# The opening of a two-block transformer kernel: five feature groups run together in place of four, modulation blocks in two banks, the first block loaded ahead of the tokens

## The chip, the cores and the metric

The kernel runs on one core of a Trainium2 chip. The metric is the device time of one execution in microseconds; for the kernel before, three runs gave a median of 2280.69 us (2280.24 to 2281.05).

## The reference

Two blocks of a small transformer are computed one after the other on 256 tokens of width 1024, with 256 context tokens beside them, all in float32. The change lies in the first steps of the first block:

```
silu_c, silu_cc = silu(c), silu(c_ctx)
mod_x = silu_c @ w_mod + b_mod            # shift, scale and gate, 3 x 1024
mod_c = silu_cc @ w_mod + b_mod           # the same for the context
hn = rms_norm(h) * gain * (1 + scale) + shift      # for tokens and context
proj = hn @ w_in                          # q, k, v, two small gates, z, u, z_pool
qkv = silu(short_conv(qkv)); q, k = l2_norm(q), l2_norm(k)
... a gated delta rule in chunks, pooling, the output product
```

After it come a second block with feed-forward layers, a short convolution and attention. None of that is touched.

## The kernel before, in words

**Data.** Tokens and context stand as `h`, 8 feature tiles (k = 0 to 7) of 128 features by 512 columns. Weights come as a stream of chunks, each of 8 tiles of 128x128, through a ring of three slots (`w_raw`). To reach float32 precision, each operand is split in a high and a low part: ScalarE casts a chunk to `w_hi` (`split_ahead`, line 867), and VectorE (for the first four chunks, `low_chunk`, line 994) or GpSimd (later, line 575) subtracts to get `w_lo`. A product of one weight tile is then three matmuls (lines 603, 604 and 607: low weights by high tokens, high by high, high by low). The tokens are split the same way: scaled by VectorE (`nt`, line 1009), shifted and cast by ScalarE (`n_hi`, line 940), and the low part by VectorE (`n_lo`, line 964).

**The modulation in the opening.** Before a feature tile k can be scaled, its shift and scale have to be known. They come in five blocks (`BLOCK_TILES`: 1, 1, 2, 2 and 2 tiles of k). Per block: SP loads the weights in two halves (`load_block`, line 467), TensorE sums them into a bank (`mod_block`, line 889), ScalarE copies the sums to `mod_row` (`copy_block`, line 930), TensorE transposes them (`turn_block`, line 898), VectorE adds the bias and forms the gain (`block_gain`, lines 978 to 987). The sums of the tokens' squares are formed beside them: squares on ScalarE and VectorE (lines 924, 955), sums on TensorE (line 905), mean and reciprocal on VectorE (lines 957, 958), square root on ScalarE (line 934), spread on TensorE (line 913).

**The groups.** The input projection ("in") makes 51 groups of output features, each the sum over the 8 tiles k. The first `IN_FIRST` groups run together, so that TensorE takes tile k for all of them before it needs tile k+1; the chunks' tiles are laid out in that order. Later groups run one at a time, 8 products each. The calls of `before(g, k)` place the modulation work among the products: for k = 0, 2 and 4, blocks 2, 3 and 4 are summed at group 2 and turned at group 3. Blocks 0 and 1 are done in `pe_start`, ahead of the products. `after(g)` is called for each group once its products are issued, or for all groups of a joint part when that part is through; it calls `post(g - POST_LAG)` with `POST_LAG = 4`. For the first eight feature tiles `post` sums squares (line 1132) and waits for `tile_sq`, which comes by way of ScalarE (line 1242), VectorE (four steps of line 1302) and ScalarE again (lines 1193 and 1198).

**Order.** Each engine runs its instructions in the order written. SP issues the transfers in the order of `sp_program`. The waits are semaphores written by hand.

Of the kernel before, what the change touches and what calls it, by code (L numbers as in the profile page):

```python
# [158 lines left out]
        self.groups, self.k = groups, k  # L159


FFN_FIRST, SC_FIRST, IN_FIRST, OUT_FIRST, MLA_FIRST = 4, 5, 4, 6, 4


def mark_plan():
# [57 lines left out]
def two_block_kernel(nc, stream, modstream, tokens, ctx2, conds, cols_in, consts_in, rope_tab, count_in, out):  # L223
# [271 lines left out]

    def sp_program(sp):
        sp.dma_start(cond[:], conds[:]).then_inc(cond_in, 16)
        for part in range(2):
            sp.dma_start(h[:, 4 * part:4 * part + 4, :], tokens[:, 4 * part:4 * part + 4, :]).then_inc(tokens_in[part], 16)
        sp.dma_start(cols[:], cols_in[:]).then_inc(const_in, 16)  # L500
        sp.dma_start(consts[:, 0:2, :], consts_in[:, 0:2, :]).then_inc(const_in, 16)
        load_block(sp, 0)
        load_chunk(sp, 0, 0)
        load_block(sp, 1)
        load_chunk(sp, 1, 1)
        load_block(sp, 2)
        load_chunk(sp, 2, 2)
        load_block(sp, 3)
        sp.wait_ge(w_lo_ready, 1)
        load_chunk(sp, 3, 0)  # L510
        load_block(sp, 4)
        stream_loads(sp, FIRST_LOWS, 2 * RING)
        sp.dma_start(consts[:, 2:, :], consts_in[:, 2:, :]).then_inc(masks_in, 16)
        sp.dma_start(inv_cnt[:], count_in[:]).then_inc(masks_in, 16)
        stream_loads(sp, 2 * RING, IN_LOADS)
        sp.wait_ge(normed, KT)
        sp.dma_start(h[:, :, L:T], ctx2[:]).then_inc(ctx2_in, 16)


        sp.wait_ge(mod_used, MOD_EARLY)  # L520
        for r in range(MOD_LATE - MOD_EARLY):
            if r == 3:
                sp.wait_ge(w_lo_ready, IN_LOADS)
            if r >= RECUR_RING:
                sp.wait_ge(mod_used, MOD_EARLY + r - RECUR_RING + 1)
            load_mod(sp, MOD_EARLY + r)


        sp.wait_ge(mod_used, MOD_LATE)
        for i in range(IN_LOADS, IN_LOADS + RING):  # L530
            load_chunk(sp, i, i % RING)
        sp.wait_ge(d_o, 8)
        for q in range(7):
            load_late(sp, q)
        stream_loads(sp, IN_LOADS + RING, CH_OUT + 10)
        sp.wait_ge(y_lo_ready, 8)
        for q in (7, 8):
            load_late(sp, q)
        stream_loads(sp, CH_OUT + 10, CH_OUT + 12)
        q = LATE_RING  # L540
        for i in range(12, 16):
            load_late(sp, q)
            q += 1
            stream_loads(sp, CH_OUT + i, CH_OUT + i + 1)
        stream_loads(sp, CH_OUT + 16, CH_FFN[0] + RING)
        for q in range(q, MOD_PARTS):
            load_late(sp, q)
        q = MOD_PARTS


        at = CH_FFN[0] + RING
        for first, after, turn in ((CH_FFN[0], CH_SC, ("sc", 0)), (CH_SC, CH_FFN[1], ("ffn", 1)),
                                   (CH_FFN[1], CH_FFN[2], ("ffn", 2)), (CH_FFN[2], CH_MLA, ("mla", 0))):
            stream_loads(sp, at, first + 12)
            at = first + 12
            for _ in range(sum(LATE_TURNS[turn][:3])):
                load_late(sp, q)
                q += 1
                stream_loads(sp, at, at + 1)
                at += 1  # L560
        stream_loads(sp, at, CH_MLA + RING)
        at = CH_MLA + RING
        for n in (1, 2, 5):
            for _ in range(n):
                load_late(sp, q)
                q += 1
            stream_loads(sp, at, at + 1)
            at += 1
        assert MOD_LATE + q == MOD_END
        stream_loads(sp, at, N_STREAM)  # L570
# [298 lines left out]

    def block_room_turned(b):  # L870

        room = bank[(MOD_BANK, 4, 5, MOD_BANK, 4)[b]]
        at = (0, 0, 0, L, L)[b]
        return room[:, at:at + P], room[:, at + P:at + 2 * P]

    def block_row(b):
        at = b % 4 * P
        return mod_row[:, at:at + P]

    def mod_block(pe, b):  # L880

        pe.wait_ge(mod_full[b], 32)
        n = BLOCK_TILES[b]
        sums, _ = block_room_turned(b)
        for k in range(KT):
            for half_ in range(2):
                for sub in range(n):
                    q = 2 * half_ + (sub if n == 2 else k % 2)
                    last = nc.tensor.matmul(sums[32 * q:32 * q + 32], cond[:, 0, k, :],
                                            block_room(b)[:, half_, k, sub * P:(sub + 1) * P],  # L890
                                            start=(k < 3 - n), stop=(k >= KT - 3 + n))
        last.then_inc(mod_used, 2 * n)
# [5 lines left out]
        nc.tensor.transpose(turned, block_row(b), C(Const.IDENT)).then_inc(mod_turned, 1)  # L898

    def pe_start(pe):  # L900
        pe.wait_ge(const_in, 16 * 2)
        for k in range(KT):
            pe.wait_ge(first_sq[k % 2], k // 2 + 1)
            for t in range(4):
                last = nc.tensor.matmul(bank[MISC_BANK][32 * t:32 * t + 32, 0:P], col(Cols.SEL + 7, 32),
                                        n_space[:, 0, k, tok(t)], start=(k == 0), stop=(k == KT - 1))
        last.then_inc(sum_ready, 1)
        pe.wait_ge(cond_ready, 1)
        mod_block(pe, 0)
        turn_block(pe, 0)  # L910
        pe.wait_ge(rstd_ready, 1)
        for t in range(4):
            last = nc.tensor.matmul(bank[MISC_BANK][:, tok(t)], C(Const.IDENT)[:, 32 * t:32 * t + 1].to_broadcast([P, P]),
                                    rstd[:, 0:P], start=True, stop=True)
        last.then_inc(rstd_spread, 1)
        mod_block(pe, 1)
        turn_block(pe, 1)

    def act_start(act):
        act.wait_ge(cond_in, 16)  # L920
        nc.scalar.activation(cond[:], cond[:], ACT.Silu).then_inc(cond_ready, 1)
        for k in range(0, KT, 2):
            act.wait_ge(tokens_in[k // 4], 16)
            nc.scalar.activation(n_space[:, 0, k, :], h[:, k, :], ACT.Square).then_inc(first_sq[0], 1)

        def copy_block(b):
            act.wait_ge(mod_used, 2 * (BLOCK_FIRST[b] + BLOCK_TILES[b]))
            if b == 4:
                act.wait_ge(mod_turned, 1)
            nc.scalar.copy(block_row(b), block_room_turned(b)[0]).then_inc(mod_copied, 1)  # L930

        nc.scalar.activation(rstd[0:1, T - 1:T], h[0:1, 0, 0:1], ACT.Sqrt, scale=0.0)
        act.wait_ge(ms_ready, 1)
        nc.scalar.activation(rstd[:, 0:P], rstd[:, 0:P], ACT.Sqrt).then_inc(rstd_ready, 1)
        copy_block(0)
        split_ahead(act, -2)
        for k in range(KT):
            act.wait_ge(scaled, k + 1)
            for c, s_ in sides(T):
                last = nc.scalar.activation(n_hi[:, k, s_], nt[:, k % 2, s_], ACT.Identity,  # L940
                                            bias=mods[:, NORMS[0][1] + k, c:c + 1])
            last.then_inc(norm_hi, 1)
            if k == 0:
                copy_block(1)
                split_ahead(act, -1)
            elif k in (1, 3, 5):
                copy_block(k // 2 + 2)
                if k > 1:
                    split_ahead(act, k // 2 - 1)

    def dve_start(dve):
        gain, shift, scale = NORMS[0]
        for k in range(1, KT, 2):
            dve.wait_ge(tokens_in[k // 4], 16)
            nc.vector.tensor_tensor(n_space[:, 0, k, :], h[:, k, :], h[:, k, :], ALU.mult).then_inc(first_sq[1], 1)
        dve.wait_ge(sum_ready, 1)
        step(nc.vector.tensor_scalar(rstd[:, 0:P], bank[MISC_BANK][:, 0:P], 1.0 / D, EPS, ALU.mult, ALU.add))
        nc.vector.reciprocal(rstd[:, 0:P], rstd[:, 0:P]).then_inc(ms_ready, 1)
        dve.wait_ge(const_in, 16 * 2)

        def low(k):
# [33 lines left out]
                                    ALU.subtract).then_inc(w_lo_ready, 1)  # L995

        for b in range(MOD_BLOCKS):
            if b >= 2:
                low_chunk(b - 1)
            block_gain(b)  # L1000
            if b == 0:
                low_chunk(0)
                dve.wait_ge(rstd_spread, 1)
            tiles = range(BLOCK_FIRST[b], BLOCK_FIRST[b] + BLOCK_TILES[b])
# [6 lines left out]
                last.then_inc(scaled, 1)  # L1011
            for k in tiles:
                low(k)


    TAIL = 1 + 3 * HEADS
# [83 lines left out]
    def pe_in(pe):  # L1100
        operands = pe_operands(pe, 0, "in", L)

        def before(g, k):
            if k in (0, 2, 4):
                if g == 2:
                    mod_block(pe, k // 2 + 2)
                if g == 3:
                    turn_block(pe, k // 2 + 2)
            if (g, k) == (IN_FIRST, 0):
                pe.wait_ge(mod_ready, MOD_BLOCKS)  # L1110
            return operands(g, k)
# [69 lines left out]
    def act_in(act):  # L1181
# [37 lines left out]
            act.wait_ge(ab_act, 3)  # L1219
            nc.scalar.activation(e_tail[:], e_tail[:], ACT.Ln, bias=1.0).then_inc(ab_act, 1)  # L1220

        split = [2]

        def split_through(i):
            while split[0] <= min(i, N_IN - 1):
# [1929 lines left out]
```

## Time and profile before

| | |
|---|---|
| median of three runs | 2280.69 us |
| the profiled execution's own time | 2278.36 us |
| its span in the trace | 2276.2 us |
| TensorE busy | 2209.8 us (97%) |
| VectorE, ScalarE, GpSimd busy | 841.8, 792.9, 1013.2 us |
| mean granted clock of TensorE | 0.995 |

The span runs from the first to the last recorded instruction of one execution. Times in the rows below count from its start. The granted clock is a share of TensorE's full speed: 1.00 stands for 2.4 GHz, 0.50 for 1.2 GHz.

### The profile page before, as it was taken

To read this page: it belongs to the slowest core of one execution; us is meant where nothing else is said; L and a number is where in the kernel's file an instruction comes from. 1 tells how busy PE (TensorE), PEld (TensorE's weight loads), DVE (VectorE), ACT (ScalarE), POOL (GpSimd) and SP (SyncE) were. 2 spreads that over 40 slices of the span, in tenths; PEclk is the share of its full clock that TensorE was granted. 3 is DMA by queue.
4 is the path that set the end of the run, shared out by engine and by line. 5 is a ranking of instruction groups with operands and counts; after the bars stand their busy time and mean duration, and the time that the engine had idled before them with its cause. 6 is when DMAs were issued, how large, how long until landed. Compare 5 with 4: busy or idle time off the path is not lost.

```text
span 2276.2 us, 37013 instructions
## 1 busy us (share of the span) xinstructions
PE 2209.8 (97%) x14686; PEld 1796.9 (79%) x14686; DVE 841.8 (37%) x1519; ACT 792.9 (35%) x1264; POOL 1013.2 (45%) x469
## 2 busy tenths in 40 slices
PE   6999999989999999999999999999999999899999
PEld 5789867778778888878878888887888887658999
DVE  4566556565511311344471131133122114662212
ACT  3445434433432132232233222223222222555443
POOL 0357622344344444434444444443444443305888
PEclk9999999999999999999999999999999999999999
DMA  8235476355443223325325323332433324304556
GB/s 284 93 103 158 134 265 218 142 200 187 175 150 118 93 93 94 99 76 175 94 70 168 104 93 93 94 97 80 171 94 93 93 93 133 105 19 122 185 185 185
DMA packets 90930, 297.55 MB, mean 131 GB/s; under 512 B 8992, under 2 KB 21664, under 8 KB 90400
## 3 DMA queue, kind: packets, MB, share of 16 engines
q1 hardware_dynamic: 90640, 295.05, 39.7%
q8 instruction: 117, 1.92, 0.3%
q10 hardware_dynamic: 144, 0.34, 0.1%
q14 instruction: 29, 0.24, 0.0%
HBM read 294.31 MB, written 1.05 MB: 130 GB/s over the span
## 4 chain that ended last, share of the span: by engine, by line
issue 55%; POOL 23%; PE 16%; DVE 2%; DMA 1%; ACT 1%; SPq 1%; POOLq 1%; DVEq 0%; ACTq 0%
POOL w_lo L575 23%; PE bank L603 3%; PE bank L607 3%; PE bank L604 3%; PE bank L647 2%; PE bank L1642 1%; PE bank L1653 1%; DVE gdn_outer L2012 1%; PE bank L1621 1%; PE bank L1095 1%; PE bank L1558 1%; DMA first_mods<-in_modstream 1%; DMA mod_raw<-in_modstream 0%; DVE gdn_outer L2014 0%; PE bank L1665 0%
## 5 line engine op out<-in xcount | busy, mean ns | idle before, releaser
L575 POOL TENSOR_TENSOR w_lo<-w_raw,w_hi 128x1024 fp32r<-128x1024 f32 x379 | 922.6, 2438 | 1083.6 <-ACT w_hi L867 1083.2
L603 PE MATMUL bank<-n_hi,w_lo 128*128 128x512 f32 (+1 forms) x2216 | 789.2, 356 | 9.0 <-POOL w_lo L575 5.5
L607 PE MATMUL bank<-n_lo,w_hi 128*128 128x512 f32 (+1 forms) x2216 | 781.8, 353 | 1.5 <-DVE n_lo L778 1.3
L604 PE MATMUL bank<-n_hi,w_hi 128*128 128x512 f32 (+1 forms) x2216 | 781.0, 352 | 0.0
L867 ACT CAST w_hi<-w_raw 128x1024 fp32r<-128x1024 f32 x383 | 401.2, 1049 | 757.8 <-PE bank L607 732.5
L603 PEld LDWEIGHTS bank<-n_hi,w_lo 128*128 128x128 f32 x2216 | 415.9, 188 | 87.2 <-issue 14.3
L607 PEld LDWEIGHTS bank<-n_lo,w_hi 128*128 128x128 f32 x2216 | 415.9, 188 | 67.9 <-DVE n_lo L778 2.5
L604 PEld LDWEIGHTS bank<-n_hi,w_hi 128*128 128x128 f32 x2216 | 416.1, 188 | 62.9
L2409 DVE TENSOR_TENSOR prod<-silu,bank 128x512 f32<-128x512 f32 (+1 forms) x88 | 54.7, 622 | 717.3 <-PE bank L607 710.1
L603 PE MATMUL bank<-g_hi,w_lo 128*128 128x512 f32 (+1 forms) x768 | 283.3, 369 | 2.1 <-DVE g_lo L2400 2.1
L607 PE MATMUL bank<-g_lo,w_hi 128*128 128x512 f32 (+1 forms) x768 | 283.3, 369 | 0.0
L604 PE MATMUL bank<-g_hi,w_hi 128*128 128x512 f32 (+1 forms) x768 | 282.8, 368 | 0.0
L2368 DVE SCALAR_TENSOR_TENSOR h<-bank,gates,h 128x256 f32<-128x256 f32 x136 | 60.7, 480 | 314.5 <-PE bank L607 314.5
L603 PEld LDWEIGHTS bank<-g_hi,w_lo 128*128 128x128 f32 x768 | 144.0, 188 | 29.7 <-DVE g_lo L2400 2.5
L604 PEld LDWEIGHTS bank<-g_hi,w_hi 128*128 128x128 f32 x768 | 144.0, 188 | 27.2
L607 PEld LDWEIGHTS bank<-g_lo,w_hi 128*128 128x128 f32 x768 | 144.0, 187 | 27.2
L2354 ACT ACTIVATE silu<-bank 128x512 f32<-128x512 f32 (+1 forms) x88 | 47.8, 544 | 287.6 <-PE bank L607 287.6
L2400 DVE TENSOR_TENSOR g_lo<-prod,g_hi 128x512 fp32r<-128x512 f32 (+1 forms) x88 | 84.7, 964 | 2.4 <-ACT g_hi L2344 2.2
L1302 DVE SCALAR_TENSOR_TENSOR conv<-bank,cols,conv 128x508 f32<-128x508 f32 (+3 forms) x96 | 63.0, 659 | 49.5 <-ACT conv L1242 46.9
L1944 POOL TENSOR_TENSOR gdn_t<-gdn_inner,consts 128x256 f32<-128x256 f32 x16 | 11.7, 728 | 137.5 <-DVE gdn_inner L1997 137.5
L847 DVE TENSOR_TENSOR nt<-h 128x512 f32<-128x512 f32 (+1 forms) x56 | 58.2, 1039 | 1.9
L832 ACT ACTIVATE n_hi<-nt,mods 128x256 fp32r<-128x256 f32 x88 | 40.3, 503 | 39.3 <-DVE nt L791 39.3
(385 smaller groups left out, 1878.8 us busy)
## 6 DMA issues: line engine op xcount, KB each, us to landing
w_raw<-in_stream SPq DMA_DIRECT2D x383, 512.0 KB, 3.6
late<-in_modstream SPq DMA_DIRECT2D x56, 512.0 KB, 4.5
mod_raw<-in_modstream SPq DMA_DIRECT2D x48, 512.0 KB, 6.0
w_raw<-in_modstream SPq DMA_DIRECT2D x48, 512.0 KB, 6.1
first_mods<-in_modstream SPq DMA_DIRECT2D x6, 1024.0 KB, 11.0
h<-in_tokens SPq DMA_DIRECT2D x2, 1024.0 KB, 6.3
first_mods<-in_modstream SPq DMA_DIRECT2D x4, 512.0 KB, 8.2
consts<-in_consts SPq DMA_DIRECT2D x1, 1152.0 KB, 5.8
```

The source lines that it names most:

```text
L575: nc.gpsimd.tensor_tensor(w_lo[:, slot, :], w_raw[:, slot, :], w_hi[:, slot, :].bitcast(F32), ALU.subtract).then_inc(w_lo_ready, 1)
L603: nc.tensor.matmul(out_ap, wl, hi, start=start, stop=False)
L604: nc.tensor.matmul(out_ap, wh, hi, start=False, stop=False)
L607: return nc.tensor.matmul(out_ap, wh, lo, start=False, stop=stop)
L647: last = nc.tensor.matmul(bank[MOD_BANK][32 * j:32 * j + 32, :], cond[:, which, k, :], room[:, jj * 512:(jj + 1) * 512], start=(k == 0), s ...
L847: square = nc.vector.tensor_tensor(nt[:, k % 2, s_], h[:, k, s_], h[:, k, s_], ALU.mult)
L867: nc.scalar.copy(w_hi[:, c % RING, :], w_raw[:, c % RING, :]).then_inc(w_hi_ready, 1)
L1302: ins = nc.vector.scalar_tensor_tensor(acc[:, :, to], src[:, :, of], col(Cols.CONV + ci * CONV + j), acc[:, :, to], ALU.mult, ALU.add)
L2354: nc.scalar.activation(silu[:, f % 2, 0:w], bank[(g0 + g) % BANKS][:, 0:w], ACT.Silu).then_inc(gate_ready, 1)
L2368: last = nc.vector.scalar_tensor_tensor(h[:, d, s_], bank[g % BANKS][:, s_], gates[:, gate, d, c:c + 1], h[:, d, s_], ALU.mult, ALU.add)
L2400: nc.vector.tensor_tensor(g_lo[:, f, 0:w], prod[:, f % 2, 0:w], g_hi[:, f, 0:w].bitcast(F32), ALU.subtract).then_inc(hid_lo, 1)
L2409: nc.vector.tensor_tensor(prod[:, f % 2, 0:w], silu[:, f % 2, 0:w], bank[g % BANKS][:, 0:w], ALU.mult).then_inc(groups_read, 2)
```

## The change

The first joint part of the projection takes five groups in place of four. In SP's order, block 0 goes ahead of the small constants, and both ahead of the tokens. The modulation blocks alternate between banks 6 and 5, in two halves of each. TensorE sums and turns block 0 before the sums of squares; ScalarE copies it before its squares, and VectorE forms its gain before its squares. Block 1 goes from `pe_start` to the joint part: blocks 1 to 4 are summed at group 2 and turned at group 4 of k = 0, 1, 3 and 5. From block 2 on, TensorE waits for the gain of the block two before. ScalarE casts chunks 1 to 4 at k = 0, 2, 4 and 5, chunk 1 before the copy of block 1; chunk 4's cast comes from the part after. VectorE's `low_chunk` calls stand at the end of a block in place of the start of the next, which is the same order.

```
-FFN_FIRST, SC_FIRST, IN_FIRST, OUT_FIRST, MLA_FIRST = 4, 5, 4, 6, 4
+FFN_FIRST, SC_FIRST, IN_FIRST, OUT_FIRST, MLA_FIRST = 4, 5, 5, 6, 4
...
     def sp_program(sp):
         sp.dma_start(cond[:], conds[:]).then_inc(cond_in, 16)
+        load_block(sp, 0)
+        sp.dma_start(cols[:], cols_in[:]).then_inc(const_in, 16)
+        sp.dma_start(consts[:, 0:2, :], consts_in[:, 0:2, :]).then_inc(const_in, 16)
         for part in range(2):
             sp.dma_start(h[:, 4 * part:4 * part + 4, :], tokens[:, 4 * part:4 * part + 4, :]).then_inc(tokens_in[part], 16)
-        sp.dma_start(cols[:], cols_in[:]).then_inc(const_in, 16)
-        sp.dma_start(consts[:, 0:2, :], consts_in[:, 0:2, :]).then_inc(const_in, 16)
-        load_block(sp, 0)
         load_chunk(sp, 0, 0)
...
-        room = bank[(MOD_BANK, 4, 5, MOD_BANK, 4)[b]]
-        at = (0, 0, 0, L, L)[b]
+        room = bank[(MOD_BANK, IN_FIRST)[b % 2]]
+        at = b // 2 % 2 * L
...
+    BLOCK_STEPS = (0, 1, 3, 5)
+
     def mod_block(pe, b):
 
         pe.wait_ge(mod_full[b], 32)
+        if b >= 2:
+            pe.wait_ge(mod_ready, b - 1)
...
     def pe_start(pe):
+        pe.wait_ge(cond_ready, 1)
+        mod_block(pe, 0)
         pe.wait_ge(const_in, 16 * 2)
+        turn_block(pe, 0)
...
         last.then_inc(sum_ready, 1)
-        pe.wait_ge(cond_ready, 1)
-        mod_block(pe, 0)
-        turn_block(pe, 0)
         pe.wait_ge(rstd_ready, 1)
...
         last.then_inc(rstd_spread, 1)
-        mod_block(pe, 1)
-        turn_block(pe, 1)
...
             if k == 0:
+                split_ahead(act, -1)
                 copy_block(1)
-                split_ahead(act, -1)
             elif k in (1, 3, 5):
                 copy_block(k // 2 + 2)
-                if k > 1:
-                    split_ahead(act, k // 2 - 1)
+                if k == 5:
+                    split_ahead(act, 2)
+            elif k in (2, 4):
+                split_ahead(act, k // 2 - 1)
...
         def before(g, k):
-            if k in (0, 2, 4):
+            if k in BLOCK_STEPS:
                 if g == 2:
-                    mod_block(pe, k // 2 + 2)
-                if g == 3:
-                    turn_block(pe, k // 2 + 2)
+                    mod_block(pe, BLOCK_STEPS.index(k) + 1)
+                if g == 4:
+                    turn_block(pe, BLOCK_STEPS.index(k) + 1)
```

## Rows read from the trace of the kernel before

**Rows 1.** The page's part 1: engine, busy us, share of the span, instructions.
```profile
PE 2209.8 (97%) x14686; PEld 1796.9 (79%) x14686; DVE 841.8 (37%) x1519; ACT 792.9 (35%) x1264; POOL 1013.2 (45%) x469
```

**Rows 2.** Timeline of TensorE, opening: start us, us, line, operation, count, idle before.
```profile
10.08 3.64 PE L905 MATMUL bank<-n_space,cols 128*32 128x128 f32 x64 [10.08 <-DMA consts<-in_consts]
...
18.41 1.08 PE L889 MATMUL bank<-first_mods,cond 128*32 128x128 f32 x32 [1.50 <-DMA first_mods<-in_modstream]
...
20.84 0.50 PE L607 MATMUL bank<-n_lo,w_hi 128*128 128x512 f32 x1
...
26.86 3.64 PE L889 MATMUL bank<-first_mods,cond 128*32 128x128 f32 x64 [4.84 <-DMA first_mods<-in_modstream]
...
31.88 0.29 PE L898 MATMUL bank<-consts,mod_row 128*128 128x128 f32 x1
...
36.99 1.96 PE L889 MATMUL bank<-first_mods,cond 128*32 128x128 f32 x64
...
52.72 0.47 PE L603 MATMUL bank<-n_hi,w_lo 128*128 128x512 f32 x1 [0.45 <-ACT n_hi L940]
...
53.88 0.40 PE L603 MATMUL bank<-n_hi,w_lo 128*128 128x512 f32 x1
...
58.78 0.39 PE L603 MATMUL bank<-n_hi,w_lo 128*128 128x512 f32 x1
...
64.48 1.06 PE L1132 MATMUL bank<-act_out,cols 128*32 128x128 f32 x8
```

**Rows 3.** Stretches: from:to, us, busy us of each engine, PEclk, DMA share, GB/s.
```profile
25.60:31.80 6.20, 4.94 (x67) 4.03 (x68) 0.00 (x0) 0.27 (x1) 0.00 (x0) 0.50 1.09 354
1971.00:1974.00 3.00, 2.48 (x12) 2.19 (x11) 2.96 (x2) 2.60 (x8) 3.00 (x2) 0.50 0.03 11
2091.40:2094.40 3.00, 3.00 (x25) 3.00 (x26) 0.37 (x1) 1.32 (x3) 3.00 (x2) 1.00 0.56 161
```

**Rows 4.** The chain of waits, opening: the issue of block 0's second half.
```profile
3.98 2.78 SPq L467
```

**Rows 5.** DMA issues from 6.7 to 6.9 us: size, us from issue to landing.
```profile
first_mods<-in_modstream SPq DMA_DIRECT2D x1, 512.0 KB, 9.6
```

**Rows 6.** Timeline of VectorE, opening.
```profile
9.02 1.29 DVE L955 TENSOR_TENSOR n_space<-h 128x512 f32<-128x512 f32 x2 [1.22 <-DMA h<-in_tokens]
13.79 0.29 DVE L957 TENSOR_SCALAR rstd<-bank 128x128 f32<-128x128 f32 x1 [3.48 <-PE bank L905]
...
16.92 1.22 DVE L994 TENSOR_TENSOR w_lo<-w_raw,w_hi 128x1024 fp32r<-128x1024 f32 x1
18.06 0.87 DVE L1009 SCALAR_TENSOR_TENSOR nt<-h,gains,bank 128x256 f32<-128x256 f32 x2
...
20.96 0.23 DVE L983 TENSOR_TENSOR mods<-bank,mods 128x2 f32<-128x2 f32 x2
...
32.20 0.23 DVE L978 TENSOR_TENSOR mods<-bank,cols 128x4 f32<-128x4 f32 x2 [6.85 <-PE bank L898]
...
50.23 0.22 DVE L978 TENSOR_TENSOR mods<-bank,cols 128x4 f32<-128x4 f32 x2
...
52.61 1.68 DVE L964 SCALAR_TENSOR_TENSOR n_lo<-nt,mods,n_hi 128x256 fp32r<-128x256 f32 x4 [0.20 <-ACT n_hi L940]
```

**Rows 7.** Timeline of ScalarE, opening.
```profile
15.53 1.05 ACT L867 CAST w_hi<-w_raw 128x1024 fp32r<-128x1024 f32 x1
...
51.66 1.71 ACT L940 ACTIVATE n_hi<-nt,mods 128x256 fp32r<-128x256 f32 x4 [2.61 <-DVE nt L1009]
...
56.88 0.68 ACT L1235 ACTIVATE gb<-bank,cols 64x512 f32<-64x512 f32 x1 [1.62 <-PE bank L607]
...
62.10 0.64 ACT L1198 ACTIVATE act_out<-kT 128x512 f32<-128x512 f32 x1
```

**Rows 8.** Timeline of TensorE, two waits in later stages.
```profile
1970.59 0.54 PE L603 MATMUL bank<-c_hi,w_lo 128*128 128x256 f32 x1 [1.88 <-ACT n_space L2740]
...
2091.38 0.39 PE L603 MATMUL bank<-n_hi,w_lo 128*128 128x256 f32 x1 [2.46 <-POOL w_lo L575]
```

More of the change, by code:

```diff
@@ L921, in act_start @@
         nc.scalar.activation(cond[:], cond[:], ACT.Silu).then_inc(cond_ready, 1)
-        for k in range(0, KT, 2):
-            act.wait_ge(tokens_in[k // 4], 16)
-            nc.scalar.activation(n_space[:, 0, k, :], h[:, k, :], ACT.Square).then_inc(first_sq[0], 1)
         def copy_block(b):
@@ L930, in copy_block @@
             nc.scalar.copy(block_row(b), block_room_turned(b)[0]).then_inc(mod_copied, 1)
+        copy_block(0)
+        for k in range(0, KT, 2):
+            act.wait_ge(tokens_in[k // 4], 16)
+            nc.scalar.activation(n_space[:, 0, k, :], h[:, k, :], ACT.Square).then_inc(first_sq[0], 1)
         nc.scalar.activation(rstd[0:1, T - 1:T], h[0:1, 0, 0:1], ACT.Sqrt, scale=0.0)
@@ L934, in act_start @@
         nc.scalar.activation(rstd[:, 0:P], rstd[:, 0:P], ACT.Sqrt).then_inc(rstd_ready, 1)
-        copy_block(0)
         split_ahead(act, -2)
@@ L943, in act_start @@
             if k == 0:
+                split_ahead(act, -1)
                 copy_block(1)
-                split_ahead(act, -1)
             elif k in (1, 3, 5):
                 copy_block(k // 2 + 2)
-                if k > 1:
-                    split_ahead(act, k // 2 - 1)
+                if k == 5:
+                    split_ahead(act, 2)
+            elif k in (2, 4):
+                split_ahead(act, k // 2 - 1)
     def dve_start(dve):
         gain, shift, scale = NORMS[0]
[L953 to L958, printed above, removed]
         dve.wait_ge(const_in, 16 * 2)
@@ L997, in dve_start @@
         for b in range(MOD_BLOCKS):
-            if b >= 2:
-                low_chunk(b - 1)
             block_gain(b)
             if b == 0:
+                for k in range(1, KT, 2):
+                    dve.wait_ge(tokens_in[k // 4], 16)
+                    nc.vector.tensor_tensor(n_space[:, 0, k, :], h[:, k, :], h[:, k, :], ALU.mult)\
+                        .then_inc(first_sq[1], 1)
+                dve.wait_ge(sum_ready, 1)
+                step(nc.vector.tensor_scalar(rstd[:, 0:P], bank[MISC_BANK][:, 0:P], 1.0 / D, EPS, ALU.mult, ALU.add))
+                nc.vector.reciprocal(rstd[:, 0:P], rstd[:, 0:P]).then_inc(ms_ready, 1)
                 low_chunk(0)
@@ L1013, in dve_start @@
                 low(k)
+            if 1 <= b < FIRST_LOWS:
+                low_chunk(b)
     TAIL = 1 + 3 * HEADS
@@ L1220, in decay_and_beta @@
             nc.scalar.activation(e_tail[:], e_tail[:], ACT.Ln, bias=1.0).then_inc(ab_act, 1)
-        split = [2]
+        split = [3]
         def split_through(i):
```

## The prediction

> **What bounds the kernel now.** I read the page's busy times first, then TensorE's timeline over the first 66 us beside those of ScalarE and VectorE, then the chain of waits and the granted clock of short stretches. TensorE is busy for 2209.8 of 2276.2 us [rows 1]: whatever makes it stand anywhere comes out at the end, and no other engine has less slack. The change touches only the opening, so the question is how long TensorE stands before it has finished the groups that run together, against now.
>
> Now its first matmul starts at 10.08, on the arrival of the constants. A product is three matmuls of 512 columns; the third one of the first product starts at 20.84. After two products TensorE stands for 4.84 us until the third modulation block (tiles 2 and 3) has arrived at 26.86, and the granted clock then is 0.50, the 1.2 GHz level [rows 2, 3]: 6.20 us at that level cost about 3.1. From 31.88 to 52.72 the listing has only waits of half a microsecond, such as the 0.45 before k=6 at 52.72. Second product of k=6: 53.88; joint part over, fifth group begins: 58.78; seven products lie between, 0.70 us each [rows 2]. From there TensorE runs without a gap worth naming.
>
> I take 53.88 as the mark. By then 25 products and all blocks are done. With five groups the same point (second product of k=6) has 31 products behind it, so 53.88 + 6 × 0.70 = 58.1 would be neutral: the total of products is unchanged.
>
> **Start.** Block 0 goes ahead of the tokens on SP's queue. The issue of its second half took 2.78 us at 3.98, and that half landed 9.6 us after its start, at 13.6 [rows 4, 5]. The bytes up to there are the same in either order, so in the new order the second half of the tokens lands at about 13.6 where VectorE has it at 9.02 now [rows 6]. The constants also pass behind block 0, but have landed before the tokens. If the 2.78 us issue holds the tokens back as well, up to 0.6 more; I take 0. Then come VectorE's two squares (1.29 in all), one k of sums at the early pace (10.08 row: 64 matmuls in 3.64, so 8 in 0.46) and a handover: the mean square starts at 15.4, now 13.79. What followed it now was the square root, the row copy of block 0, and the cast of chunk 0 at 15.53 [rows 7]; without the copy (0.16 of that) the cast starts at 17.0. It takes 1.05, the low half and the scaled tokens follow 1.14 apart as now (16.92 to 18.06), so the scaling starts at 19.2, 1.14 later than now. The gain of block 0 leaves this chain, but the tokens, now last, are in it. The first product's third matmul moves from 20.84 to 22.0 and the second product ends at 23.0.
>
> Sums and turn of block 1 (1.08 us and some 0.3 as at 31.88) lay before the first product; they now lie inside k=0. ScalarE's cast of chunk 1 (1.05) is put before the copy of block 1; it would hold that up only if the chunk landed after 23.0, at worst with block 2, which is behind it in SP's queue, at 26.86 (3.9 us). I take nothing, since two 1 MB halves lie between. The other casts, the low halves on VectorE (same order as now) and the new wait for the gain of block b-2 (products queue behind it, but that gain is two blocks old) I cost at nothing too; one exception below.
>
> **The blocks.** This is the first term. From turn to use: turn at 31.88, bias add on VectorE at 32.20; later block, bias add at 50.23, first product at 52.72: 0.32 + 2.49 = 2.81 us, with nothing else on those engines in the way [rows 2, 6]. A block of one tile adds twice: 0.26 more (20.96 row). The first product after such a wait takes 1.16 (52.72 to 53.88) as its third matmul waits for the low half. Now a block summed at k=2 is used at k=4, a whole k later, and the chain is hidden but for 0.45. In the new order blocks 1, 2, 3, 4 are summed in k=0, 1, 3, 5 at the third group and turned at the fifth, and used in the next k. After the turn there is one product (0.7) to hide 2.81.
>
> Step by step, blocks of two tiles 1.96 [rows 2]: block 1 summed by 24.1, two products to 25.5, turn, k=1 starts at 25.5 + 3.07 = 28.6 (TensorE free at 26.3: 2.2 lost). 1.16 + 0.70 + 2.0 + two products: turn of block 2 at 33.8, k=2 at 36.6 (1.95 lost). The wait for block 2's bytes at 26.86 is over by then, covered by the five products that came forward. Then 1.16 + 6 × 0.70 + 2.0 + 1.4: turn at 45.3, k=4 at 48.15 (2.0 lost). In k=4 chunk 3 is needed already by the last product: ScalarE's cast (1.05) now stands between the tiles 4 and 5, then comes tile 5 (half of 1.71), its low half (half of 1.68) and the low half of the chunk (1.22) [rows 6, 7]: ready at 52.1, needed at 51.4, 0.7 lost. k=6 starts at 60.4 (2.0 lost) and its second product at 61.6. Against 58.1: 3.5 us later.
>
> **After the joint part.** This is the second term. The work on the length sums of feature tile 0 (line 1132) is put four groups behind, so it comes after group 4. Group 4 was a group of its own: 5.6 us of products hid the way through ScalarE, VectorE and ScalarE. With five together group 4 ends with the joint part, and the sums are the next thing on TensorE. Now group 0 is read at 56.88 and the square that they need ends at 62.10 + 0.64 = 62.74 [rows 7], 3.96 us after the joint part's end at 58.78; with one group more behind group 0 that is 0.70 less, so TensorE stands for 3.3 us. At present this work starts at 64.48 [rows 2], long after. Its own 1.0 us is paid either way. I find no later stage that would give the 3.3 back: TensorE is the last there.
>
> **The clock.** What the trace doesn't show is TensorE's clock under the new waits. Early work now comes in pieces with gaps (block 0, four sums, four sums, spread), so the first two products and block 1 may run at 1.2 GHz: 0 to 2 × 0.70 + 1.08 = 2.5 more; I take 1.2, having no row nearer to one end. Later: after the wait of 1.88 us before 1970.6 the stretch 1971 to 1974 was granted 0.50, after the one of 2.46 before 2091.38 the next 3 us had 1.00 [rows 3, 8]. So a wait of about two microseconds can go either way, at 1.5 us a time. Of five waits (2.2, 1.95, 2.0, 2.0, 3.3) I take two to be punished, 3.0 us; the ends are 0 and 7.5. A gain isn't in it: the 3.1 us that the low clock costs now is already counted as saved, since the neutral mark uses the real 53.88.
>
> The Trainium skill, in "TensorE: Matmul & The Clock Gate" (Why this matters for your kernels), asks for no long idle gaps between bursts of matmuls, else the engine is back at half rate. The trace bears it out partly: 4.84 us brought 0.50, but 1.88 did so too and 2.46 did not. By that rule only the wait after the joint part would be punished, and the sum would be 1.5 us lower.
>
> **Sum.** 3.5 + 3.3 + 1.2 + 3.0 = 11.0 us slower. Bounds: 6.8 with the clock at nothing, 6.8 + 2.5 + 7.5 = 16.8 with all of it. The profiled execution took 2278.36 (span 2276.2 and 2.2 around it), 2.3 below the median 2280.69 of the runs; I add the sum to the median: 2291.7.
>
> **Rivals.** *No penalty from the clock*: +6.8, 2287.5. For it: the 2.46 us wait with 1.00 after it; against: the 1.88 one. *Every wait punished*: +16.8, 2297.5. *The blocks come out even*: the covered 4.84 us wait and the 3.1 us of low clock pay for the new waits, and only the 3.3 after the joint part remains: 2284.0. For it: ScalarE and VectorE have little else to do then, so a chain could be shorter by overlap; against: four waits of 2 us would have to shrink by 3.5 in all. *Not slower*: the place is the way from a turned block to the first product of the next k. If the waits there (8.15 us in all) vanish, the sum of both terms is 6.8 - 8.15, so 2279.3; it decides from a chain of about 0.8 us, what one product covers. Against it are its parts: two scalings of 0.45, two biased casts of 0.45 and a pair of adds and gains, each waiting for the one before; 2.49 us stand in the row with nothing in between. That loading ahead doesn't bring the first product forward is no rival but part of the sum.
>
> **Chances.** Forecast with one to four punished waits 0.45; no penalty 0.22; all punished 0.12; blocks even 0.12; not slower 0.09. A measurement here tells about 0.2% (4.6 us) from no change: under 2276.1 faster, over 2285.3 slower. The forecast and the first two rivals are slower (0.79) with a fifth of "blocks even" (0.02): 0.81. The rest of that (0.10) and over half of "not slower" (0.05) lie within: 0.15; faster 0.04. The range 2283.5 to 2297 leaves out "not slower" and the far end of "all punished"; the forecast's own is 2288.5 to 2295.
>
> **What would show it.** Right: TensorE waits of about 2 us on ScalarE's n_hi before k=1, 2, 4 and 6 and no wait of 4 us or more on a modulation block; a wait of about 3 us on the square at line 1132's sums between the joint part and group 5, which is absent now; tokens landing near 13.6 and the third matmul of the first product near 22. Wrong: k=6's second product before 58.1 or no wait ahead of group 5. The clock's term is read from the granted clock after each of these waits.

## The result and the profile after

The changed kernel takes 2294.53 us (median of five runs, 2292.05 to 2300.47) against 2281.05 for the kernel before: a ratio of 1.0066, interval 1.0053 to 1.0079. It is slower by 13.5 us; 11.0 were forecast, with 2283.5 to 2297 as the range. The profiled execution is the slowest of the five, 2300.47 us with a span of 2298.3; it lies 5.9 us above the median, so what its trace shows of the loss is more than the median has.

The page's busy times of the changed kernel (engine, busy us, share, instructions), answering to [rows 1]: TensorE runs the same number of instructions and is busy for 9 us longer, so part of its matmuls ran slower.

```profile
PE 2219.0 (97%) x14686; PEld 1800.7 (78%) x14686; DVE 846.1 (37%) x1519; ACT 792.7 (34%) x1264; POOL 1013.5 (44%) x469
```

TensorE's timeline in the opening of the changed kernel, answering to [rows 2]: the waits (us and releaser in brackets).

```profile
14.73 1.93 PE L912 MATMUL bank<-n_space,cols 128*32 128x128 f32 x32 [0.51 <-ACT n_space L934]
...
18.41 2.08 PE L917 MATMUL bank<-rstd,consts 128*128 128x128 f32 x8 [1.74 <-ACT rstd L937]
...
22.48 0.76 PE L603 MATMUL bank<-n_hi,w_lo 128*128 128x512 f32 x1 [2.00 <-ACT n_hi L942]
...
32.16 0.50 PE L603 MATMUL bank<-n_hi,w_lo 128*128 128x512 f32 x1 [2.00 <-ACT n_hi L942]
...
40.31 0.50 PE L603 MATMUL bank<-n_hi,w_lo 128*128 128x512 f32 x1 [1.74 <-ACT n_hi L942]
...
53.48 0.51 PE L603 MATMUL bank<-n_hi,w_lo 128*128 128x512 f32 x1 [1.74 <-ACT n_hi L942]
...
57.28 0.50 PE L603 MATMUL bank<-n_hi,w_lo 128*128 128x512 f32 x1 [0.28 <-DVE w_lo L992]
...
67.30 0.79 PE L603 MATMUL bank<-n_hi,w_lo 128*128 128x512 f32 x1 [3.38 <-ACT n_hi L942]
...
80.19 1.92 PE L1137 MATMUL bank<-act_out,cols 128*32 128x128 f32 x8 [3.13 <-ACT act_out L1203]
```

No wait on a modulation block's bytes is left after the first products; in its place stand the four waits on `n_hi` before k = 1, 2, 4 and 6, and the one before the length sums. The second product of k=6 starts here:

```profile
68.81 0.63 PE L603 MATMUL bank<-n_hi,w_lo 128*128 128x512 f32 x1
```

That is 10.7 us past the neutral 58.1. The granted clock of stretches of the changed kernel (from:to, us, busy us of each engine, PEclk), answering to [rows 3]:

```profile
42.10:45.30 3.20, 3.20 (x9) 2.52 (x8) 1.96 (x3) 0.00 (x0) 0.00 (x0) 0.50 0.14 28
66.00:72.40 6.40, 5.10 (x12) 3.85 (x13) 3.45 (x9) 3.69 (x6) 3.26 (x2) 0.50 0.30 82
79.60:86.40 6.80, 6.21 (x18) 4.72 (x19) 6.55 (x10) 4.41 (x8) 0.00 (x0) 0.50 0.01 2
```

16.4 us at 1.2 GHz in the opening, against 6.2 before. Where a loss to the low clock is named below, it is half of the time granted 0.50 up to 120 us, with the waits in it counted as well, so that it is an upper bound: 8.5 us here, 3.4 in the kernel before. And one thing that I had not looked for: VectorE's timeline at the gain of block 4, and GpSimd's beside it, both of the changed kernel.

```profile
63.26 0.23 DVE L976 TENSOR_TENSOR mods<-bank,cols 128x4 f32<-128x4 f32 x2 [6.04 <-PE bank L902]
63.53 1.87 DVE L985 SCALAR_TENSOR_TENSOR gains<-mods,cols 128x2 f32<-128x2 f32 x2
```

```profile
62.95 2.36 POOL L575 TENSOR_TENSOR w_lo<-w_raw,w_hi 128x1024 fp32r<-128x1024 f32 x1 [62.50 <-ACT w_hi L867]
```

Two gain instructions take 1.87 us where those of block 3 take 0.23; they end at 65.40, GpSimd at 65.31. This makes the wait before k=6 3.38 and not 1.74.

A mark that every kernel here passes is the first transpose of the value tiles, in the middle of the stage; from it to the last of them it is 36.0 or 36.1 us in each. Kernel before, then the changed one:

```profile
L1123 PE MATMUL bank<-consts,act_out x32: 270/272/300, 118.7 to 154.7; 128*128 128x128 f32 x32
```

```profile
L1128 PE MATMUL bank<-consts,act_out x32: 270/272/301, 137.2 to 173.2; 128*128 128x128 f32 x32
```

18.5 of the 22.1 us by which this execution's span is longer lie before the mark. Of the other 3.6, 3.2 have come by the first spread at line 742 (607.8 us before, 629.5 now).

### The profile page after: what moved, and what is told of

Read it like the earlier page. It is cut to its first block, busy times and chain, and to the rows that moved or that the text cites. A ratio compares the mean times of both kernels' runs of the same rounds, so it can differ in the third digit from the quotient of the medians.

```text
span 2298.3 us, 37013 instructions
## 1 busy us (share of the span) xinstructions
PE 2219.0 (97%) x14686; PEld 1800.7 (78%) x14686; DVE 846.1 (37%) x1519; ACT 792.7 (34%) x1264; POOL 1013.5 (44%) x469
## 4 chain that ended last, share of the span: by engine, by line
issue 55%; POOL 23%; PE 17%; DVE 2%; ACT 1%; DMA 1%; POOLq 1%; SPq 0%; DVEq 0%; ACTq 0%
POOL w_lo L575 23%; PE bank L603 3%; PE bank L607 3%; PE bank L604 3%; PE bank L647 2%; PE bank L1647 1%; PE bank L1658 1%; DVE gdn_outer L2017 1%; PE bank L1626 1%; PE bank L1100 1%; PE bank L1563 1%; DMA h<-in_tokens 0%; DVE gdn_outer L2019 0%; PE bank L1670 0%; POOLq L580 0%
## 5 line engine op out<-in xcount | busy, mean ns | idle before, releaser
L847 DVE TENSOR_TENSOR nt<-h 128x512 f32<-128x512 f32 (+1 forms) x56 | 58.1, 1038 | 1.9
```

Source lines behind the costliest of these rows:

```text
L847: square = nc.vector.tensor_tensor(nt[:, k % 2, s_], h[:, k, s_], h[:, k, s_], ALU.mult)
```

## The experiments

The theory: the loss is the chain from a block's turn to the next k with one product to hide it, the bare wait before the length sums, the later start, and the low clock behind the waits. The rivals: late bytes, five groups as such, a wait that is merely pushed on.

**The length sums after group 5** (e1).

```
         def after(g):
-            if 0 <= g - POST_LAG < 24:
+            if g == IN_FIRST:
+                post(0)
+            if 1 <= g - POST_LAG < 24:
                 post(g - POST_LAG)
```

> The changed kernel with one edit: the length sums of feature tile 0 are issued after group 5 in place of directly after the joint part. Theory (a wait of 3.1 us for the square stands bare between the joint part and group 5, and the clock falls behind it): the wait is gone from the trace, 3.1 us and some 1.5 to 3 of low clock with it, so 2288.5 to 2291.5 against 2294.5 of the changed kernel. Rival (the wait is only pushed on, to the sums of tile 1 or the banks of groups 6 to 8): a new wait of about 3 us within the next four groups and 2294 or more.

2291.97 us, ratio 1.0049 (1.0036 to 1.0063). TensorE goes through without a wait, and no new one follows in the next groups; the first two sums stand together:

```profile
81.61 1.94 PE L1137 MATMUL bank<-act_out,cols 128*32 128x128 f32 x16
```

The wait isn't pushed on. The time is just outside what was expected: 2.6 us below the changed kernel, where the wait alone is 3.1, and the two intervals overlap, so it is the trace that shows the wait gone, not the time. This execution lost 8.5 us to the low clock before 120 us, as much as the changed kernel's, at other places: from 19.5 us on, before the first product, and behind the waits before k = 2, 4 and 6.

**The blocks placed otherwise** (e2). Besides the lines shown, block 1 stands at the end of `pe_start` again, and `copy_block(1)` ahead of `split_ahead(act, -1)`.

```
-    BLOCK_STEPS = (0, 1, 3, 5)
+    BLOCK_STEPS = (1, 2, 4)
...
                 if g == 2:
-                    mod_block(pe, BLOCK_STEPS.index(k) + 1)
-                if g == 4:
-                    turn_block(pe, BLOCK_STEPS.index(k) + 1)
+                    mod_block(pe, BLOCK_STEPS.index(k) + 2)
+                if g == 3:
+                    turn_block(pe, BLOCK_STEPS.index(k) + 2)
```

> The changed kernel with the blocks placed otherwise: block 1 summed and turned ahead of the products as in the kernel before; blocks 2, 3 and 4 summed at group 2 and turned at group 3 of k = 1, 2 and 4, so that two of them are used a whole k later. Theory (the chain from the turn to the next k, 2.8 us with one product to hide it, makes the waits): the waits before k=1, 4 and 6 go, that before k=2 stays at about 1.4; with block 1 out of the joint part 1.9 + 2.2 + 2.2 + 2.2 and some 2 us of low clock are saved: 2283 to 2287. Rival (the waits come from five groups as such, the chunks or the bytes of the blocks): waits of the same length with other releasers, 2292 to 2296.

2280.52 us, ratio 0.9998 (0.9989 to 1.0007): 14 us below the changed kernel, more than expected. All of the waits in its opening after the first product, and a stretch of the granted clock:

```profile
34.27 0.50 PE L603 MATMUL bank<-n_hi,w_lo 128*128 128x512 f32 x1 [1.04 <-ACT n_hi L944]
...
35.19 0.50 PE L607 MATMUL bank<-n_lo,w_hi 128*128 128x512 f32 x1 [0.18 <-DVE n_lo L964]
...
63.49 1.92 PE L1139 MATMUL bank<-act_out,cols 128*32 128x128 f32 x8 [3.15 <-ACT act_out L1205]
```

```profile
34.30:62.00 27.70, 25.87 (x220) 20.03 (x220) 15.42 (x36) 12.86 (x21) 7.21 (x3) 1.00 0.68 232
```

Three of four waits are gone and the fourth is 0.70 shorter, which makes 7.8 us; the gain of block 4 isn't held up, and the clock stays at 1.00 up to the length sums. What the other 6 us are was not tried apart; the loss to the low clock is 3.4 us in place of 8.5, and block 1's sums now stand where TensorE waited 2.00 us for the first product. Five groups as such don't bring the waits.

**The old start** (e3): SP's order, and the order of `pe_start`, `act_start` and `dve_start` up to the square root, as in the kernel before; the rest as changed.

```
         sp.dma_start(cond[:], conds[:]).then_inc(cond_in, 16)
-        load_block(sp, 0)
-        sp.dma_start(cols[:], cols_in[:]).then_inc(const_in, 16)
...
         for part in range(2):
...
+        sp.dma_start(cols[:], cols_in[:]).then_inc(const_in, 16)
...
+        load_block(sp, 0)
         load_chunk(sp, 0, 0)
```

> The changed kernel with the start of the kernel before: tokens ahead of block 0 on SP's queue, sums of squares ahead of block 0 on TensorE, and the same order on ScalarE and VectorE; block 1 and the rest as in the changed kernel. Theory (block 0 ahead of the tokens makes the first product late): the third matmul of the first product comes at about 21 in place of 23.5, and 1.1 to 2.6 us are saved: 2292 to 2293.5. Rival (loading block 0 ahead pays, what follows makes the loss): 2294.5 to 2297.

2297.38 us, ratio 1.0071 (1.0057 to 1.0085). That is not what I expected, yet not what the rival says either: its products start earlier, at 21.45 against 22.48 (the third matmul of the first at 22.27 against 23.47), and k=1 at 30.16 against 32.16, but the clock falls five times (8.5 us lost before 120 us). Its interval overlaps that of the changed kernel, so the time can't tell this edit; the pair e5 and e6 below tries it with the waits out of the way.

**The turn one product earlier** (e4).

```
-                if g == 4:
+                if g == 3:
                     turn_block(pe, BLOCK_STEPS.index(k) + 1)
```

> The changed kernel with one edit: blocks 1 to 4 are turned at group 3 in place of group 4, one product earlier. Theory (the waits before k = 1, 2, 4 and 6 are the chain from the turn on): each is 0.70 us shorter, four times, 2.8 us, and with shorter waits the clock can only gain: 2289.5 to 2292. Rival (the waits end on something else than the turn: bytes, casts of chunks, the banks): no wait is shorter, 2294.5.

2289.29 us, ratio 1.0035 (1.0022 to 1.0048), just under what was expected, with an interval clear of the changed kernel's. The four waits, on TensorE's timeline:

```profile
29.89 0.50 PE L603 MATMUL bank<-n_hi,w_lo 128*128 128x512 f32 x1 [1.30 <-ACT n_hi L942]
...
37.33 0.50 PE L603 MATMUL bank<-n_hi,w_lo 128*128 128x512 f32 x1 [1.03 <-ACT n_hi L942]
...
48.27 0.51 PE L603 MATMUL bank<-n_hi,w_lo 128*128 128x512 f32 x1 [1.03 <-ACT n_hi L942]
...
59.77 0.50 PE L603 MATMUL bank<-n_hi,w_lo 128*128 128x512 f32 x1 [1.02 <-ACT n_hi L942]
```

2.00, 1.74 and 1.74 became 1.30, 1.03 and 1.03: 0.70 each, one product. The waits are the chain from the turn on, not bytes. The fourth lost 2.36, since the gain now came 0.12 us before GpSimd started. And no low clock was seen before the length sums.

**Both cures together** (e5 with the old start, e6 with the changed start): the edits of e1 and e2 in one kernel.

> Five groups together, with the start order of the kernel before (tokens first, sums of squares before block 0), block 1 ahead of the products, blocks 2 to 4 summed at k = 1, 2, 4 and turned at group 3, and the length sums of tile 0 after group 5. Theory (the placing of the blocks and of the length sums is the loss, and five groups as such hide the wait for block 2): 2270 to 2276, faster than the kernel before. Rival (five groups as such cost something that the earlier runs left in): 2279 or more. Beside the next kernel it tells what the start order alone is worth once nothing else waits: 1 to 2.5 us faster than that one if block 0 ahead of the tokens costs, not faster if the earlier run with the old start (slower by 3 us) told the truth.

> The same as the kernel just before, but with the changed start order (block 0 ahead of the tokens, and first on each engine). Theory: against the run with the blocks alone placed otherwise (2280.5) the 3.15 us wait before the length sums and the 3.4 us of low clock that follow it go: 2273 to 2277. Rival (that wait only moves): 2279 to 2281.

2274.29 us, ratio 0.9969 (0.9958 to 0.9980), and 2274.56 us, ratio 0.9975 (0.9966 to 0.9984): both beat both kernels, by some 0.3% against the one before. The intervals overlap, so the start order is worth less than these runs tell apart. In the traces the product of k=2 starts at 33.10 with the old start and at 33.78 with the changed one, and the mark, the first transpose of the value tiles, comes at 113.0 and at 113.7 (118.7 in the kernel before): 0.7 us in one execution of each. From there e5 runs to 72 with 0.2 us of idle time:

```profile
33.10:72.00 38.90, 38.71 (x283) 30.64 (x284) 26.23 (x51) 21.26 (x34) 9.63 (x4) 1.00 0.51 177
```

**Filling matmuls in the last wait** (e7): the changed kernel with

```
+            if g == POST_LAG:
+                for _ in range(3):
+                    nc.tensor.matmul(bank[MISC_BANK][:, 0:448], C(Const.IDENT), cols[:, 0:448], start=True, stop=True)
             if 0 <= g - POST_LAG < 24:
                 post(g - POST_LAG)
```

> The changed kernel with one addition: three matmuls of 448 float32 columns into a bank that is read by nobody, directly ahead of the length sums after the joint part, so that TensorE works through most of its wait of 3.13 us. They are no part of the computation. Theory (the clock falls because TensorE stands, and costs beside the wait): the sums start at the same distance from the joint part's end, no stretch at 0.50 follows them, and 1.5 to 3.4 us are saved: 2291 to 2293. Rival (the clock falls for another reason, or costs nothing there): 2294.5 or more.

2295.74 us, ratio 1.0065 (1.0049 to 1.0081). The time is the rival's. In the trace the sums wait for 0.88 us more only, and the 6.8 us from there on are granted 1.00, where the first profile of the changed kernel has 0.50.

```profile
79.80:86.60 6.80, 6.80 (x33) 5.23 (x34) 6.55 (x10) 4.41 (x7) 0.00 (x0) 1.00 0.01 4
```

That isn't the filling's doing for certain: in e9 below, the changed kernel once more, the same wait without filling was followed by 1.00 too. TensorE's sums and a later stretch of e9:

```profile
80.48 1.06 PE L1137 MATMUL bank<-act_out,cols 128*32 128x128 f32 x8 [3.13 <-ACT act_out L1203]
```

```profile
82.00:83.00 1.00, 1.00 (x6) 0.78 (x5) 0.96 (x3) 0.83 (x2) 0.00 (x0) 1.00 0.06 16
```

And in e7 the clock still fell behind three earlier waits (5.1 us lost). So this run settles nothing on the clock; e11 and e12 do.

**Chunk 4 cast earlier** (e8, and once more as e10 beside e9, the changed kernel again).

```
+                if k == 5:
+                    split_ahead(act, 2)
                 copy_block(k // 2 + 2)
-                if k == 5:
-                    split_ahead(act, 2)
```

> The changed kernel with one edit: at k=5 ScalarE casts chunk 4 before it copies block 4's sums, not after, so that GpSimd's low half of chunk 4 is over some 4 us before VectorE forms the gain of block 4. Theory (the gain, which reads two operands in SBUF, stands still while GpSimd works: 1.87 us for two instructions that take 0.23 otherwise): the gain takes 0.23 again, the wait before k=6 falls from 3.38 to 1.74 us, and 1.6 us and more of low clock are saved: 2290 to 2293. Rival (the slow gain is something else, such as the fetch of instructions): it stays at 1.9 us, 2294.5.

> The changed kernel itself once more, to stand beside the next three on the same chip: its runs so far spread from 2292 to 2300. Theory (the spread is the clock, which falls after some of the waits and not after others): again 2292 to 2300, with another set of stretches at 0.50 in the opening than before.

> The kernel with chunk 4 cast ahead of the copy of block 4 once more, beside the changed kernel on the same chip (its first runs were slower, 2298.6, though its trace had the gain back at 0.23 us). Theory (1.64 us of waiting saved, which the clock's play can hide): the wait before k=6 is 1.74 again, the time 0 to 4 us below the changed kernel's. Rival (the earlier cast costs elsewhere): 2 to 4 us above it.

e8 2298.62 (ratio 1.0079, 1.0063 to 1.0094); e9 2295.09 (2293.4 to 2303.2; ratio 1.0061, 1.0045 to 1.0077); e10 2295.47 (ratio 1.0064, 1.0050 to 1.0077). In e8, GpSimd's work, VectorE's gain of block 4, and TensorE's wait before k=6:

```profile
57.31 2.37 POOL L575 TENSOR_TENSOR w_lo<-w_raw,w_hi 128x1024 fp32r<-128x1024 f32 x1 [56.86 <-DVE w_lo L992]
```

```profile
64.51 0.23 DVE L985 SCALAR_TENSOR_TENSOR gains<-mods,cols 128x2 f32<-128x2 f32 x2
```

```profile
66.64 0.50 PE L603 MATMUL bank<-n_hi,w_lo 128*128 128x512 f32 x1 [1.74 <-ACT n_hi L942]
```

The hold-up is what it was taken for: with GpSimd out of the way the gain takes 0.23 and the wait 1.74, or 1.75 in e10. In time the 1.6 us don't show against e9. At the mark they do; e9, then e10, which both lost 5.1 us to the low clock before 120 us:

```profile
L1128 PE MATMUL bank<-consts,act_out x32: 270/272/300, 134.7 to 170.7; 128*128 128x128 f32 x32
```

```profile
L1128 PE MATMUL bank<-consts,act_out x32: 270/273/299, 133.0 to 169.0; 128*128 128x128 f32 x32
```

e10 is 1.7 us ahead there. Where the kernels are the same, after the mark, two executions differ by more: e9's profiled execution passes it 2.5 us ahead of the first profile of the changed kernel and still takes 2.8 us longer.

**Filling matmuls in all five waits** (e11), and with chunk 4 cast earlier (e12): besides e7's, before each of k = 1, 2, 4 and 6, into a half (`free`) of bank 6 or 5 that has been read

```
+            if g == 0 and k in (1, 2, 4, 6):
+                pe.wait_ge(mod_ready, {1: 1, 2: 2, 4: 3, 6: 2}[k])
...
+                for _ in range(3):
+                    nc.tensor.matmul(free, C(Const.IDENT), cols[:, 0:L], start=True, stop=True)
```

> The changed kernel with matmuls that are no part of the computation in its five waits: three of 256 float32 columns before each of k = 1, 2, 4 and 6, into halves of banks that hold nothing any more, and three of 448 before the length sums after the joint part. All fit in the waits. Theory (each wait that lets the clock fall costs 1.7 us more behind it): no stretch at 0.50 in the opening behind the joint part's first product, the waits end where they did, and against the changed kernel 3 to 8 us are saved: 2288 to 2292. Rival (the clock costs nothing of note in the opening): within 1.5 us of the changed kernel.

> Both edits together: the filling matmuls, and chunk 4 cast ahead of the copy of block 4. With the clock held up, what GpSimd costs VectorE's gain can be seen alone. Theory: 1.6 us less than with the filling alone, so 2286 to 2290.5, and only the chain's waits (four of about 2 us and the 3.1 us one) and the later start are left over the kernel before. Rival (the gain's hold-up is hidden): the same time as with the filling alone.

2289.53 us, ratio 1.0034 (1.0021 to 1.0046), and 2290.29, ratio 1.0034 (1.0022 to 1.0047). Beside their twins without filling, e11 saves 5.6 us (against e9) and e12 5.2 us (against e10), and no product comes earlier by the filling itself: k=1 starts at 32.13 in e11 and at 32.02 in e9. What is saved is the clock. In e11 it still fell once, behind the wait before k=6 that GpSimd makes longer than the filling is; in e12 the profile shows no low clock before 118 us, as between k=1 and k=6:

```profile
29.00:64.00 35.00, 32.17 (x300) 23.63 (x298) 15.74 (x45) 8.88 (x19) 2.39 (x1) 1.00 0.60 207
```

The mark in e11 and in e12, and the second product of k=6 in e12:

```profile
L1134 PE MATMUL bank<-consts,act_out x32: 270/272/301, 131.9 to 167.9; 128*128 128x128 f32 x32
```

```profile
L1134 PE MATMUL bank<-consts,act_out x32: 270/272/299, 129.1 to 165.1; 128*128 128x128 f32 x32
```

```profile
65.30 0.39 PE L603 MATMUL bank<-n_hi,w_lo 128*128 128x512 f32 x1
```

So the waits, the start and the early slow matmuls alone put the mark 10.4 us later than before. Up to the mark the filling saves 2.8 us (e9 to e11) and 3.9 us (e10 to e12), less than the medians say; the rest would lie after the mark, where nothing was edited and executions of one kernel differ by as much. So the clock in the opening costs 3 to 6 us, and these runs don't say it closer. The cast's 1.6 us don't show between the medians of e11 and e12 either; at the mark e12 is 2.8 us ahead, the cast and one fall of the clock less.

## Why the prediction was right

**The start: right in kind, too small.** The last tokens came at 14.05, 13.6 were forecast. But I let only one k of sums follow the squares; TensorE did four at the slow pace (14.73, 1.93 us), so the mean square started at 16.73 and not 15.4. The spread was slow as well (2.08 us for 8). The first product started at 22.48 and its matmuls ran some 0.43 us apart, the pace of the stretches at 0.50, until 28.2, though the granted clock in the profile reads 1.00 there. The third matmul of the first product came at 23.47 and not 22.0, and all this put k=1 at 32.16 where 28.6 was worked out: 3.6 us, of which the sum had 1.2. This term is the one that was sized too small by most.

**The blocks: right.** From k=1 to k=2 8.15 us (8.0 worked out). From k=2 to k=4 13.17 (11.55): the rest is the low clock from 42.1 to 45.3. The waits were 2.00, 1.74 and 1.74 for 2.2, 1.95 and 2.0, and the one for chunk 3's low half 0.28 for 0.7. e4 showed the chain by moving the turn by one product, e2 by taking three of the waits away. Without low clock and without the term below, in e12, the second product of k=6 starts at 65.30, 7.2 us past the neutral 58.1: the 3.5 us of the blocks and the 3.6 of the start.

**One term was missing.** I costed the earlier cast of chunk 4 at nothing. It lets GpSimd start its low half just when block 4 is turned, and VectorE's gain stands 1.64 us until GpSimd is through. The kernel before had GpSimd's first work at 54.46, after the last gain. The Trainium skill, in "SBUF — State Buffer" (Who interferes with whom), says that a VectorE instruction with two inputs in SBUF contends with a GpSimd instruction that reads SBUF, for a port pair that is locked exclusively, and that the order of issue decides who waits. The trace agrees: the bias add, with one input in PSUM, took its usual 0.23 while GpSimd worked, and the gain, with both inputs in SBUF, ended 0.09 us after it; in e4, where the gain came 0.12 us before GpSimd, it took 0.23.

**The length sums: right.** 3.13 us for 3.3, and e1 took the wait away whole.

**The clock: right in kind, its size open.** Two punished waits were taken, 3.0 us; in this execution three stretches (behind or in the waits of 1.74, 3.38 and 3.13) were at 0.50, 16.4 us in all, with TensorE at work for 14.5 of them. e11 and e12 give a price of 5.6 and 5.2 us by the medians, of 2.8 and 3.9 by the mark, so 3.0 is at the low end. Which waits are punished differs between executions of one kernel, and their length alone doesn't decide it, since 1.74 us was punished and the 3.13 us of e9 was not: the changed kernel, e9 and e7 differ only after the joint part or not at all, and had 8.5, 5.1 and 5.1 us of loss before 120 us. The kernel before isn't free of such play: beside e5 to e8 its runs went from 2276.4 to 2286.7.

**Rivals.** "Blocks even" fell with the four waits. It had counted 3.1 us for the low clock before; of that stretch of 6.20 us TensorE worked 4.94, so 2.5 is nearer. "Not slower" needed chains near 0.8 us; they are 2.7 (turn at 37.60, k=2 at 40.31). "No penalty" comes closest to e12: 2290.3, more than the 2287.5 it was given, by the start. The cover itself worked: the 4.84 us wait for block 2 is gone, and with the blocks and the length sums placed to suit, the same five groups are 6 us faster than four.

**The sum.** By the traces the terms come to more than was forecast: 3.6 for the start in place of 1.2, and 1.6 for the gain in place of nothing, which would make the 11.0 into 15.0. The medians show 13.5. Part of the difference may be that the kernel before was profiled in an execution 2.3 us under its median; this wasn't tried. That the time lies inside the range is in part luck: two of the five runs, 2297.9 and 2300.47, lie above its end at 2297.

**Left open:** the start order's own worth (under what e5 and e6 tell apart), and the 3.2 us between the mark and line 742's first spread in the profiled execution; both kernels fall to the low clock for a while between 530 and 630 us, and it wasn't tried what sets that.

## What to carry to other kernels

When a joint part gets wider, look up everything that was counted in groups: a lag "four groups later" had been 5.6 us of cover and became none. When work is moved nearer to its use to wait less for bytes, work out the chain from it to the use and count the products that are left between. And give TensorE's waits the price of the clock behind them: here 3 to 6 us on top of 12.0 us of waits (2.00, 1.74, 1.74, 3.38 and 3.13).

## What the runs showed of the hardware

- The same wait was followed by 0.50 in one execution and not in another: the 1.74 us before k=2 was in the changed kernel (the stretch from 42.1), the 1.74 before k=4 was not there but was in e8 and e9 (55.2 to 58.4 in both); the 2.00 before k=1 was in e3 (32.0 to 35.4) and not in the changed kernel; the 3.13 before the length sums was in the changed kernel and not in e9. With matmuls of no use in all five waits, and the gain not held up, the profile of e12 shows 1.00 from 7 to 118 us.
- Between 22.5 and 28.2 us of the changed kernel matmuls of 512 columns ran 0.43 us apart while the profile gives the granted clock as 1.00; in e1 such a stretch is given as 0.50 (19.5 to 26).
- VectorE's gain of block 4 (two inputs in SBUF) took 1.87 or 1.88 us where GpSimd's subtraction in SBUF had started before it (the changed kernel, e1, e3, e7, e9, e11), and 0.23 us where GpSimd wasn't at work or started after it (the kernel before, e2, e4, e5, e6, e8, e10, e12).
